# The even token mixer of a two-layer decoder trunk: one projection stream with heads and groups at fixed places

## The chip, the core and the metric

One of the eight cores of a Trainium2 chip runs the whole program. The metric is the device time of one execution in microseconds, the median of several runs; less is better. The engines are named PE (TensorE: matmuls, with PEld for its weight loads), DVE (VectorE), ACT (ScalarE), POOL (GpSimd) and SP (SyncE, which starts the weight DMAs). Each runs its own instructions in the order written and waits on semaphores for the others.

## The reference, cut to what matters

Tokens: 512. Width: 1024. The residual stream `x` passes six sub-layers, each `x += post(f(pre(x)))` with RMS norms: FFN, even mixer, FFN, FFN, odd mixer, FFN. The change touches the even mixer:

```python
q, k, v, g, a_low, z, xbc, dt = split(h @ w_in)
log_a = log_sigmoid(a_low @ w_gate2 + b_gate2) / 16
o = gla_chunked(q * 128**-0.5, k, v, log_a)          # 4 heads, key 128, value 256
o = rmsnorm(o, gla_norm) * silu(g)                   # per head
xbc = silu(causal_conv4(xbc)); xs, B, C = split(xbc) # 4 groups of 4 SSD heads of 64
dt = softplus(dt + dt_bias); a = -exp(a_log)
y = ssd_chunked(xs * dt, dt * a, B, C) + d * xs
y = rmsnorm(y * silu(z), ssm_norm)                   # per group of 256 columns
return concat([o, y]) @ w_out
```

All in float32. Both recurrences are computed in closed form over four blocks of 128 tokens, with decays `exp(b_i - b_j)`.

## The kernel before, in words

**Weights.** Every weight matrix is cut into slots of 128x1024. SP loads slot n into one of three `raw` buffers, ACT rounds it to `w_hi` (`split_high`, line 417), and DVE or POOL writes `w_lo = raw - w_hi` (`split_low`, lines 1231 and 354). PE forms each product as three matmuls (hi·hi, hi·lo, lo·hi) in the fast float32 format, `products` (line 784) with the weights stationary, `token_products` (line 793) with the weights moving. In the mixers a slot's split pair lies in a ring of four buffers (`INNER`), so slot n can be split once PE has finished slot n-4; elsewhere the ring has six. PE waits for `lo_done` before each slot. One slot of 24 matmuls with 512 columns is eight steps of three matmuls.

**The even mixer.** 49 slots are projected (`plan_stages`, line 52): 9 of `qk_small` (the small one holds `a_low` and `dt`), 8 of `v`, 16 of `xbc`, 16 of `zg`, and then 16 slots of `even_out`. PE does `first_four`, the rest of `qk_small`, `v`, `turn_dt` (line 951), then `gla_heads` (line 963) with the 16 `xbc` slots cut between the small products of four heads, `ssm_groups` (line 1011) with the 16 `zg` slots between those of four groups, and `sublayer_out` (line 848). `tiles_of` (line 895) deals the big matmuls: `project(2)` is two of the eight steps. A projected tile is copied from PSUM by DVE (`take`), and PE may not start the tile after the next before that. A head has seven levels of decays; level j needs DVE `differences(j)`, ACT `decay_of(j)`, DVE `factors(j)`, four PE matmuls and DVE `merge(j)`. The outputs of heads and groups are features x tokens, so that their norm needs sums over partitions: ACT squares, a DVE add, PE `norm_sums` (line 804), DVE mean, POOL power -0.5, a DVE diagonal, PE `norm_spread` (line 810), a DVE copy. POOL makes `w_lo` of all 49 slots from the fifth of the mixer to the fourth of `even_out`, in its own order, with the powers between (line 383). After the last group ACT and DVE split the 16 rows of the mixer's output into `cat_hi` and `cat_lo` (lines 566 and 1428), and PE starts `even_out` on them.

**The other sub-layers** run FFN slots back to back, with a `boundary` between two of them in which norms and transposes of one token chunk lie beside the matmuls of the next.

Of the kernel before, what the change touches and what calls it, by code (L numbers as in the profile page):

```python
# [7 lines left out]
F32 = mybir.dt.float32  # L8
# [24 lines left out]
DT0 = 32  # L33
# [18 lines left out]
def plan_stages():  # L52

    ffn = [[(f"gate_up{f}", 2 * FT), (f"down{f}", FT)] for f in range(N_FFN)]
    even = [("qk_small", 2 * GH + 1), ("v", 8), ("xbc", 16), ("zg", 16), ("even_out", 16)]
    odd = [("latent", 6), ("q_up", 5), ("k_up", 2), ("v_up", 2), ("odd_out", 8)]
    stages, first = {}, 0
    for name, slots in ffn[0] + even + ffn[1] + ffn[2] + odd + ffn[3]:
        stages[name] = (first, slots)
        first += slots  # L60
    return stages, first

def plan_ring(stages, total):
# [6 lines left out]
    for name in ("qk_small", "v", "xbc", "zg", "latent", "q_up", "k_up", "v_up"):  # L71
        inner |= set(range(stages[name][0], sum(stages[name])))
# [12 lines left out]
def plan_norms():  # L85

    names = [("gla", h) for h in range(GH)] + [("ssm", g) for g in range(SG)] + ["q_latent", "kv_latent"]
    return {name: n for n, name in enumerate(names)}

def build_trunk(nc, dram, out):
# [8 lines left out]
    with ExitStack() as ctx:  # L100
# [23 lines left out]
        v_head = [temps[:, 5 + c // 2, (c % 2) * GDV:(c % 2) * GDV + GDV] for c in range(NC)]  # L124
        diag = other[1].rearrange("p (c t) -> p c t", c=NC)

        gain_pre = sb("gain_pre", [P, D])
        mixer_misc, = parts(("mixer_misc", 1, D, F32))
        gain_post = sb("gain_post", [P, D])
        far_one, far_rest = temps[:, 7, 0:3 * P], mixer_misc[:, 0, 0:3 * P]  # L130
        far_blocks = [far_one, far_rest[:, 0:2 * P], far_rest[:, 2 * P:3 * P]]
        ssm_cols = mixer_misc[:, 0, 512:512 + 14 * SH].rearrange("p (n h) -> p n h", h=SH)

# [3 lines left out]
        mixer_cols = sb("mixer_cols", [P, 132])  # L137
# [13 lines left out]
        dt_bias = mixer_cols[DT0:DT0 + SH, 102:103]  # L151
        a_log = mixer_cols[DT0:DT0 + SH, 103:104]
# [8 lines left out]
        cat_lo, cat_hi = parts(("cat_lo", 24, T, F32R), ("cat_hi", 16, T, F32R))  # L161
# [26 lines left out]
        XS, B_ROWS, C_ROWS, Q, K, V = 0, 8, 12, 16, 20, 24  # L188
        CAT = [Q + h + m * GH for m in range(2) for h in range(GH)] + [XS + k for k in range(8)]
        small = rows(a_rows, 32)  # L190

        HALF_P = P // 2
        MASKS = len(SPANS) * HALF_P + P
        level_mask = rows(a_rows, 34)[:, 0:MASKS // 4].bitcast(U8)
        tri = rows(a_rows, 34)[:, 256:384]
        gate2 = rows(a_rows, 35)[0:RANK, :]
        LOG_A = 37
        head_rstd = rows(a_rows, 43)
        dt_rows, cum, far1, far2 = [rows(a_rows, n)[DT0:DT0 + SH, :] for n in (33, 32, 42, 43)]

        scores = rows(a_rows, 33).rearrange("p (c t) -> p c t", c=NC)
        k_dec = [rows(a_rows, 35 + b) for b in range(2)]
        conv_in = [rows(a_rows, 41 + b) for b in range(2)]

        cb = scores
        x_group = v_head
        x_far = rows(a_rows, 24, 3).rearrange("p (n v) -> p n v", n=6)
        decay = [rows(a_rows, 27 + b) for b in range(2)]
        from_start = [rows(a_rows, 29 + b) for b in range(2)]
        b_group = rows(a_rows, 31)  # L210
        xs_group = rows(a_rows, 35, 2).rearrange("p (m t) -> p m t", m=2)
        y_sum = [rows(a_rows, row) for row in (37, 39)]
        head_row = [rows(a_rows, 41 + b)[DT0:DT0 + SH, :] for b in range(2)]
# [9 lines left out]
        peak = mixer_cols[:, 112:116]  # L223
        peak_bias = mixer_cols[:, 116:120]
        prob_sum = mixer_cols[:, 120:124]
        chunk_decay = mixer_cols[:, 124:128]
        ssm_chunk_decay = mixer_cols[DT0:DT0 + SH, 128:132]
# [3 lines left out]
        SPLITS_BEFORE_NORM = {"xbc": 3, "zg": 2}  # L231
        XBC_BANKS, ZG_BANKS = (2, 3), (1, 6)
        QK0, V0, XBC0, ZG0, LATENT0 = 0, 9, 17, 33, 49

        def first_bank(n):

            return 4 + n if n < 4 else n % 4

# [19 lines left out]
        tile_taken, row_silu = sem("tile_taken"), sem("row_silu")  # L258
        conv_started, conv_step, conv_done = sem("conv_started"), sem("conv_step"), sem("conv_done")
        decay_logits, logit_ready, softplus_ready = sem("decay_logits"), sem("logit_ready"), sem("softplus_ready")  # L260
# [3 lines left out]
        key_copied, value_copied, gla_out = sem("key_copied"), sem("value_copied"), sem("gla_out")  # L264
        head_squares, head_summed = sem("head_squares"), sem("head_summed")
        dt_signal, dt_act, dt_cum, dt_far = sem("dt_signal"), sem("dt_act"), sem("dt_cum"), sem("dt_far")
        cols_turned, cols_ready = sem("cols_turned"), sem("cols_ready")
        group_copied, x_turned, x_taken, x_far_ready = sem("group_copied"), sem("x_turned"), sem("x_taken"), sem("x_far_ready")
        cb_ready, cb_taken, cb_far_taken = sem("cb_ready"), sem("cb_taken"), sem("cb_far_taken")
        head_row_ready, row_spread, from_start_ready = sem("head_row_ready"), sem("row_spread"), sem("from_start_ready")  # L270
        decay_diff, decay_exp, decay_ready = sem("decay_diff"), sem("decay_exp"), sem("decay_ready")
        y_diag_done, y_far_done, y_gated = sem("y_diag_done"), sem("y_far_done"), sem("y_gated")
        group_squares, group_summed, group_done = sem("group_squares"), sem("group_summed"), sem("group_done")
# [25 lines left out]
        ROW_BANKS = (0, 5)  # L299
        CB_AT = ((2, 0), (3, P), (5, 0), (5, 2 * P))  # L300
        FAR = [(0, 1), (1, 2), (2, 3), (0, 2), (1, 3), (0, 3)]

        @block.sync
        def _(sp):
# [9 lines left out]
            def load_gain_pre(s):  # L314
                sp.wait_ge(normed_ready, 8 * s)
                sp.dma_start(gain_pre[:, :], dram["gains"][s:s + 1, :].to_broadcast([P, D])).then_inc(gain_pre_in, 16)

            def load_gain_post(s):
                sp.wait_ge(update1_done, NC * s)
                if s == EVEN:  # L320
                    sp.wait_ge(group_done, SG)
# [9 lines left out]
            for s in range(N_SUB):  # L331
                names = [n for n in stages if first_slot[s] <= stages[n][0] < first_slot[s + 1]]
                for name in names:
                    first, slots = stages[name]
                    for n in range(RAW if first == 0 else 0, slots):
                        load(first + n, dram["w_" + name][n])
                        if first + n == first_slot[s] + 8 and s + 1 < N_SUB:
                            load_gain_pre(s + 1)
                        if s and first + n == {EVEN: last_slot[s] + 3, ODD: last_slot[s]}.get(s, first_slot[s] + 7):
# [9 lines left out]
        def _(pool):  # L349
# [27 lines left out]
            for b in range(N_SUB + 1):  # L377
# [5 lines left out]
                if b == EVEN:  # L383
                    split_some("qk_small", INNER, 9)
                    split_some("v", 0, 8)
                    split_some("xbc", 0, INNER)
                    for name, count, norm in (("xbc", GH, ("gla", 0)), ("zg", SG, ("ssm", 0))):
                        for turn in range(count):
                            for n in range(4):
                                if n == SPLITS_BEFORE_NORM[name]:  # L390
                                    power(turn + norms[norm])
                                split_low(stages[name][0] + INNER + 4 * turn + n)
# [13 lines left out]
        def _(act):  # L406
# [96 lines left out]
            def out_stage(s, ahead):  # L503

                n = last_slot[s] + ahead
                for j in range(max(2 * half_slots[s] - TAIL, half_slots[s] + 1)):
# [9 lines left out]
            def ffn(f, s):  # L516
# [8 lines left out]
                out_stage(s, RING)  # L525

            def even():
                def softplus(tile):
                    if tile == 4:
                        for h in range(GH):  # L530
                            act.wait_ge(logit_ready, h + 1)
                            after(nc.scalar.activation(other[h % 2], other[h % 2], ACT.Exp, scale=-1.0))
                            nc.scalar.activation(other[h % 2], other[h % 2], ACT.Ln, bias=1.0).then_inc(softplus_ready, 1)

                def step_sizes(tile):

                    if tile == 0:
                        act.wait_ge(dt_signal, 1)
                        nc.scalar.activation(far1, far1, ACT.Exp, scale=-1.0)
                        nc.scalar.activation(a_log, a_log, ACT.Exp).then_inc(dt_act, 1)  # L540
                    if tile == 1:
                        act.wait_ge(dt_signal, 2)
                        nc.scalar.activation(cum, far2, ACT.Ln).then_inc(dt_act, 1)
                    if tile == 2:
                        act.wait_ge(dt_cum, 1)
                        nc.scalar.activation(ssm_chunk_decay, cum[:, P - 1:T:P], ACT.Exp)
                        act.wait_ge(dt_cum, 2)
                        nc.scalar.activation(far1[:, 0:3 * P], far1[:, 0:3 * P], ACT.Exp).then_inc(dt_act, 1)

                first = first_slot[EVEN]  # L550
                for tile in range(9):
                    if tile == 8:
                        softplus(tile)
                    split_high(first + INNER + tile)
# [1356 lines left out]
```

## Time and profile before

| | |
|---|---|
| median of 3 runs | 2367.57 us (2367.52 to 2368.17) |
| the profiled execution, its own time | 2367.07 us |
| its span, and what lies around it | 2365.3 us, 1.8 us |
| busy: PE, PEld, DVE, ACT, POOL | 2239.2, 1812.3, 1009.8, 739.3, 193.0 us |
| mean granted PE clock | 0.967 |
| chain that ended last: PE, DVE, issue, ACT, POOL | 61%, 4%, 3%, 2%, 1% |
| DMA | 197.31 MB, mean 83 GB/s |

A busy PE is a PE with a matmul open; matmuls overlap, so a pace is read from the distance of two starts, not from one duration. The granted clock is 1.0 at 2.4 GHz and 0.5 at 1.2 GHz. The even mixer runs from the first matmul of its `first_four` at 387.6 us to that of the next FFN at 997.8 us.

### The profile page before, as it was taken

How to read it: one execution, taken by the hardware profiler on the slowest of the kernel's cores; microseconds unless marked ns; L12 is line 12 of the kernel's file. 1: busy time of each engine (PE TensorE's matmuls, PEld its weight loads, DVE VectorE, ACT ScalarE, POOL GpSimd, SP SyncE). 2: the span in 40 equal slices, each digit the busy share in tenths (PEclk: the TensorE clock that was granted, in tenths of full speed). 3: DMA queues.
4: the chain of work that ended last, by engine and by line, in shares of the span. 5: the costliest groups of instructions: out<-in, count | busy, mean ns of one | idle time of the engine just before them, and what ended most of it. 6: DMA issues, size and time to landing. Idle time of an engine off the chain costs nothing.

```text
span 2365.3 us, 25040 instructions
## 1 busy us (share of the span) xinstructions
PE 2239.2 (95%) x10358; PEld 1812.3 (77%) x10358; DVE 1009.8 (43%) x1438; ACT 739.3 (31%) x1141; POOL 193.0 (8%) x128
## 2 busy tenths in 40 slices
PE   7999999798888888999999999999998789999999
PEld 6888888677765666888888888888886348888887
DVE  4333224458876665443332343332265335333322
ACT  4222223433333333332221232222233434322211
POOL 0000001332212120000000000000033000000000
PEclk9999999899998889999999999999999779999999
DMA  5332332221111112242323232323222002332331
GB/s 180 95 102 89 107 98 71 79 71 45 54 36 37 43 36 101 69 134 89 107 89 107 72 125 92 104 89 107 90 83 75 15 0 71 118 106 89 107 98 54
DMA packets 55298, 197.31 MB, mean 83 GB/s; under 512 B 6272, under 2 KB 6784, under 8 KB 55184
## 3 DMA queue, kind: packets, MB, share of 16 engines
q1 hardware_dynamic: 53856, 193.75, 25.4%
q10 hardware_dynamic: 1328, 1.96, 0.2%
q8 instruction: 82, 1.34, 0.2%
q14 instruction: 32, 0.26, 0.0%
HBM read 193.58 MB, written 2.10 MB: 83 GB/s over the span
## 4 chain that ended last, share of the span: by engine, by line
PE 61%; DVE 4%; issue 3%; ACT 2%; POOL 1%; DVEq 0%; ACTq 0%; POOLq 0%
PE ps L789 11%; PE ps L790 11%; PE ps L791 11%; PE ps L797 7%; PE ps L799 7%; PE ps L798 7%; PE ps L1162 1%; PE ps L1161 1%; DVE a_rows L1226 1%; ACT a_rows L415 1%; ACT a_rows L727 1%; DVE a_rows L1223 1%; DVE temps L1223 1%; PE ps L1042 0%; PE ps L1172 0%
## 5 line engine op out<-in xcount | busy, mean ns | idle before, releaser
L789 PE MATMUL ps<-h_hi,w_hi 128*128 128x512 f32 (+1 forms) x1976 | 746.8, 378 | 12.4 <-DVE temps L1599 9.2
L791 PE MATMUL ps<-h_hi,w_lo 128*128 128x512 f32 (+1 forms) x1976 | 734.4, 372 | 0.0
L790 PE MATMUL ps<-h_lo,w_hi 128*128 128x512 f32 (+1 forms) x1976 | 733.9, 371 | 0.0
L415 ACT ACTIVATE w_hi<-raw 128x1024 fp32r<-128x1024 f32 x352 | 370.5, 1056 | 790.5 <-PE ps L799 392.4
L1223 DVE TENSOR_TENSOR w_lo<-raw,w_hi 128x1024 fp32r<-128x1024 f32 x288 | 343.7, 1221 | 338.0 <-ACT w_hi L415 337.4
L789 PEld LDWEIGHTS ps<-h_hi,w_hi 128*128 128x128 f32 x1976 | 376.4, 190 | 86.1 <-issue 21.1
L791 PEld LDWEIGHTS ps<-h_hi,w_lo 128*128 128x128 f32 x1976 | 376.2, 190 | 64.3
L790 PEld LDWEIGHTS ps<-h_lo,w_hi 128*128 128x128 f32 x1976 | 376.6, 191 | 61.8 <-issue 2.5
L1223 DVE TENSOR_TENSOR a_rows<-a_rows,ps 128x512 f32<-128x512 f32 x88 | 60.5, 688 | 614.0 <-PE ps L791 614.0
L797 PE MATMUL ps<-w_hi,a_hi 128*128 128x512 f32 x704 | 274.4, 390 | 0.0
L799 PE MATMUL ps<-w_hi,a_lo 128*128 128x512 f32 x704 | 274.0, 389 | 0.0
L798 PE MATMUL ps<-w_lo,a_hi 128*128 128x512 f32 x704 | 273.9, 389 | 0.0
L358 POOL TENSOR_TENSOR w_lo<-raw,w_hi 128x1024 fp32r<-128x1024 f32 x64 | 154.1, 2407 | 379.1 <-ACT w_hi L415 378.8
L799 PEld LDWEIGHTS ps<-w_hi,a_lo 128*128 128x128 f32 x704 | 132.1, 188 | 27.7
L798 PEld LDWEIGHTS ps<-w_lo,a_hi 128*128 128x128 f32 x704 | 132.2, 188 | 27.3
L797 PEld LDWEIGHTS ps<-w_hi,a_hi 128*128 128x128 f32 x704 | 132.1, 188 | 27.0
L520 ACT ACTIVATE a_rows<-ps 128x512 f32<-128x512 f32 x88 | 52.6, 598 | 317.6 <-PE ps L791 317.6
L371 POOL TENSOR_TENSOR stats<-stats,minus_half 128x1 f32<-128x1 f32 x24 | 13.2, 549 | 1613.8 <-DVE stats L1226 1613.8
L1223 DVE TENSOR_TENSOR a_lo<-a_rows,a_hi 128x512 fp32r<-128x512 f32 x88 | 60.3, 685 | 0.0
L1229 DVE SCALAR_TENSOR_TENSOR a_rows<-a_rows,mixer_cols 128x511 f32<-128x511 f32 (+3 forms) x61 | 54.5, 913 | 4.6 <-ACT a_rows L580 4.0
L797 PE MATMUL ps<-w_hi,cat_hi 128*128 128x512 f32 x128 | 50.7, 396 | 5.7 <-DVE cat_lo L1223 5.7
L415 ACT ACTIVATE a_hi<-a_rows 128x512 fp32r<-128x512 f32 x88 | 54.1, 615 | 0.0
(182 smaller groups left out, 1918.9 us busy)
## 6 DMA issues: line engine op xcount, KB each, us to landing
raw<-in_w_gate_up SPq DMA_DIRECT2D x176, 512.0 KB, 3.7
raw<-in_w_down SPq DMA_DIRECT2D x88, 512.0 KB, 3.5
raw<-in_w_xbc SPq DMA_DIRECT2D x16, 512.0 KB, 3.5
raw<-in_w_zg SPq DMA_DIRECT2D x16, 512.0 KB, 3.5
raw<-in_w_even_out SPq DMA_DIRECT2D x16, 512.0 KB, 3.6
raw<-in_w_qk_small SPq DMA_DIRECT2D x9, 512.0 KB, 3.5
raw<-in_w_v SPq DMA_DIRECT2D x8, 512.0 KB, 3.5
raw<-in_w_odd_out SPq DMA_DIRECT2D x8, 512.0 KB, 3.5
```

Of the source, the lines that this page charges most:

```text
L358: nc.gpsimd.tensor_tensor(w_lo[buffer_of[n]][:, 0:width], raw[n % RAW][:, 0:width], w_hi[buffer_of[n]][:, 0:width].bitcast(F32), ALU.subtr ...
L415: return nc.scalar.activation(to, source, ACT.Copy, scale=scale)
L520: nc.scalar.activation(rows(a_rows, tile), ps[:, (4 + 2 * tile) % 8, :], ACT.Silu).then_inc(silu_done, 1)
L727: nc.scalar.activation(probs[:, qt, 0:(qt + 1) * P], ps[:, qt, 0:(qt + 1) * P], ACT.Exp, bias=peak_bias[:, qt:qt + 1], scale=SCORE_SCALE, ...
L789: nc.tensor.matmul(to, w_h, hi, start=first, stop=False)
L790: nc.tensor.matmul(to, w_h, lo, start=False, stop=False)
L791: return nc.tensor.matmul(to, w_l, hi, start=False, stop=last)
L797: nc.tensor.matmul(ps[:, bank, :], hi, w_h, start=first, stop=False)
L798: nc.tensor.matmul(ps[:, bank, :], hi, w_l, start=False, stop=False)
L799: return nc.tensor.matmul(ps[:, bank, :], lo, w_h, start=False, stop=last)
L1223: return nc.vector.tensor_tensor(to, a, b, op)
L1229: return nc.vector.scalar_tensor_tensor(out=to, in0=a, scalar=scalar, in1=b, op0=op0, op1=op1)
```

## The change

The mixer's projections, and the first half of `even_out`, become one stream (a Python generator) whose steps of three 512-column matmuls are numbered: place -40 is the fifth slot of `qk_small`, 0 the first slot of `vg`, 320 the first of `even_out`, 384 its half. `plan_even` gives each head 41 places and each group 45, and each of their small products a place; `project_to(place)` runs the stream up to it. ACT and DVE ask `keep_up(place)` and so split slots, evict tiles and convolve up to that place, between the steps of heads and groups.

- The slot order is `qk_small`, `vg` (v and g by turns), `xbc` and `z` by groups. `v`, `g` and `z` are made tokens x features. `g` and `z` leave PSUM through ACT's Silu. `z2` and `z3` use matmuls of 256 columns.
- Heads and groups give tokens x features too. Their mean squares come from ACT with `accum_out`, the scale is one number per partition, and the result is transposed (eight per head or group) and split into `cat` straight from PSUM.
- The convolution reads PSUM itself: ACT writes the first tap, DVE adds three; the copies before it go.
- Each group's decays come from matmuls of `source_rows` and `head_rows` (32 rows deep) instead of `ones` times `head_row`; `skip` adds `d * xs` on PE.
- All `w_lo` of the mixer are made by DVE; POOL keeps the powers.
- The gains for the next sub-layer are loaded at slot 11 of `even_out`.

```diff
+    for h in range(GH):
+        base = 12 + 41 * h
+        for j, step in enumerate((0, 3, 7, 10, 14, 17, 22)):
+            at["level", h, j] = base + step
+        at["own", h], at["far", h], at["out", h], at["head_turn", h] = base + 25, base + 30, base + 36, base + 65
+    for g in range(SG):
+        base = 12 + 41 * GH + 45 * g
+        for name, step in (("x", 0), ("cb", 13), ("skip", 18), ("group_turn", 52)):
+            at[name, g] = base + step
+        for r in range(4):
+            at["decay", g, r] = base + (4, 9, 17, 22)[r]
+            at["near", g, r] = base + (19, 22, 27, 31)[r]
+    tile_end = [128 + 8 * (n + 1) + (32 if n >= 4 else 0) + (16 if n >= 12 else 0) for n in range(16)]
...
                 if b == EVEN:
-                    split_some("qk_small", INNER, 9)
...
+                    for n in range(GH + SG):
+                        power(n)
...
+                def split_to(place):
+                    while upcoming["slot"] < min(stream + place // 8 + 4, INNER_END):
+                        split_high(upcoming["slot"])
+                        upcoming["slot"] += 1
...
+                def keep_up(place):
+                    clear(place)
+                    for g in range(SG):
+                        if tile_end[4 * g + 1] + 3 <= place:
+                            silu_x(g)
+                        if tile_end[4 * g + 3] + 3 <= place:
+                            silu_bc(g)
+                    split_to(place)
...
+                    for j in range(len(SPANS)):
+                        keep_up(even_at["level", h, j] - AHEAD)
+                        decay_of(j)
...
+                    keep_up(max(even_at["near", g, 3] + 7, (192, 192, 272, 320)[g]))
+                    act.wait_ge(y_gated, g + 1)
...
+                        nc.scalar.activation(junk[c // 2][...], token_rows[c], ACT.Square,
+                                             scale=1.0 / 16.0, accum_out=group_sums[:, c:c + 1]).then_inc(group_squares, 1)
+                    act.wait_ge(rstd_col_ready, norms[("ssm", g)] + 1)
+                    for c in range(NC):
+                        copy(token_rows[c], token_rows[c], rstd_col[:, c:c + 1]).then_inc(y_scaled, 1)
...
+                def project_to(place):
+                    while placed[0] < place:
+                        next(projecting)
+                        placed[0] += 1
...
+                    for j in range(len(SPANS)):
+                        project_to(even_at["level", h, j])
+                        pe.wait_ge(gla_factors, h * 8 + (j + 1))
...
+                    def decays(r):
+                        n = 4 * g + r
+                        project_to(even_at["decay", g, r])
+                        pe.wait_ge(head_row_ready, n + 1)
...
+                    decays(0)
+                    project_to(even_at["x", g] + 7)
+                    turn_group(g - 1) if g else turn_head(GH - 1)
+                    decays(1)
...
+                        if j == 2 and h + 1 < GH:
+                            log_decay(h + 1)
+                        if j == 3 and h == 0:
+                            step_sizes()
...
+                    keep_up(even_at["near", g, 3] + 7)
+                    pair = token_pair.rearrange("p (c v) -> p c v", c=2)
+                    dve.wait_ge(y_far_done, g + 1)
...
+                    tt(pair, pair, z_pair(g), ALU.mult).then_inc(y_gated, 1)
+                    dve.wait_ge(group_squares, 4 * g + 4)
+                    ts(mean[:, :], group_sums, EPS, None, ALU.add).then_inc(mean_ready, 1)
```

## Rows read from the trace of the kernel before

**Rows 1.** The chain of waits by engine, from the page.
```profile
PE 61%; DVE 4%; issue 3%; ACT 2%; POOL 1%; DVEq 0%; ACTq 0%; POOLq 0%
```

**Rows 2.** Busy time by stretch: each engine's busy us and records, PE clock, DMA share.
```profile
core 0: us, PE busy (x) PEld busy (x) DVE busy (x) ACT busy (x) POOL busy (x), PEclk, DMA share, GB/s
387.60:505.00 117.40, 103.50 (x529) 86.47 (x527) 50.02 (x72) 43.91 (x52) 40.38 (x19) 0.94 0.27 85
...
509.30:692.00 182.70, 162.91 (x849) 132.84 (x850) 153.28 (x259) 60.74 (x101) 42.80 (x20) 0.95 0.15 47
692.00:907.40 215.40, 177.55 (x737) 125.06 (x735) 135.35 (x240) 74.17 (x111) 42.79 (x20) 0.87 0.12 37
907.40:997.70 90.30, 90.25 (x400) 74.85 (x401) 40.30 (x56) 30.35 (x54) 2.96 (x6) 0.98 0.30 99
387.60:997.70 610.10, 538.06 (x2541) 422.92 (x2540) 381.83 (x630) 211.45 (x322) 131.28 (x66) 0.92 0.19 59
```

**Rows 3.** PE by form, 345 to 1010 us: busy, mean ns, idle before, releaser.
```profile
L789 PE MATMUL ps<-h_hi,w_hi 128*128 128x512 f32 x296 | 131.6, 445 | 9.7 <-DVE temps L1599 9.2 <-DVE mixer_misc L1423 0.5
...
L797 PE MATMUL ps<-w_hi,cat_hi 128*128 128x512 f32 x128 | 50.7, 396 | 5.7 <-DVE cat_lo L1223 5.7
...
L976 PE MATMUL ps<-temps,a_rows 128*128 128x64 f32 x224 | 31.5, 288 | 8.2 <-DVE a_rows L1223 7.7 <-DVE a_rows L1527 0.5
...
L1042 PE MATMUL ps<-a_rows,ones 16*128 16x512 f32 x32 | 19.8, 721 | 0.0
L812 PE MATMUL ps<-temps,ones 128*128 128x512 f32 x16 | 10.9, 768 | 16.0 <-DVE temps L1223 16.0
...
L807 PE MATMUL ps<-ones,temps 128*128 128x1 f32 x64 | 8.4, 252 | 5.4 <-DVE temps L1223 5.4
```

**Rows 4.** PE's timeline: start us, duration us, what; pace of the big matmuls.
```profile
503.58 0.39 PE L797 MATMUL ps<-w_hi,h_hi 128*128 128x512 f32 x1
...
504.26 0.39 PE L797 MATMUL ps<-w_hi,h_hi 128*128 128x512 f32 x1
...
997.77 0.28 PE L789 MATMUL ps<-h_hi,w_hi 128*128 128x256 f32 x1
...
998.13 0.28 PE L789 MATMUL ps<-h_hi,w_hi 128*128 128x256 f32 x1
```

**Rows 5.** PE's timeline: the small products and what starts after them.
```profile
519.56 1.00 PE L976 MATMUL ps<-temps,a_rows 128*128 128x64 f32 x8
520.37 0.48 PE L789 MATMUL ps<-h_hi,w_hi 128*128 128x512 f32 x1
...
753.09 1.03 PE L1021 MATMUL ps<-ident,a_rows 128*128 128x128 f32 x8
753.96 2.32 PE L1025 MATMUL ps<-a_rows 128*128 128x512 f32 x8
756.04 0.48 PE L789 MATMUL ps<-h_hi,w_hi 128*128 128x512 f32 x1
...
780.69 0.71 PE L1059 MATMUL ps<-temps,a_rows 128*128 128x128 f32 x4
...
782.23 1.09 PE L1050 MATMUL ps<-a_rows,temps 128*64 128x128 f32 x8
783.25 0.50 PE L789 MATMUL ps<-h_hi,w_hi 128*128 128x512 f32 x1
```

**Rows 6.** POOL by form, 387 to 998 us.
```profile
L358 POOL TENSOR_TENSOR w_lo<-raw,w_hi 128x1024 fp32r<-128x1024 f32 x49 | 119.0, 2429 | 323.8 <-ACT w_hi L415 323.6
L367 POOL TENSOR_TENSOR rstd_col<-mean,minus_half 128x4 f32<-128x4 f32 x8 | 8.1, 1009 | 61.2 <-DVE mean L1226 61.2
```

**Rows 7.** DVE: two row operations in the timeline, and two forms.
```profile
596.65 0.68 DVE L1223 TENSOR_TENSOR temps<-ident,rstd_col 128x512 f32<-128x512 f32 x1
597.25 2.71 DVE L1226 TENSOR_SCALAR a_rows<-a_rows,mixer_cols 128x512 f32<-128x512 f32 x1
...
L1223 DVE TENSOR_TENSOR w_lo<-raw,w_hi 128x1024 fp32r<-128x1024 f32 x23 | 28.0, 1223 | 58.2 <-ACT w_hi L415 58.0
...
L1416 DVE TENSOR_TENSOR_SCAN a_rows<-ones,a_rows 128x128 f32<-128x128 f32 x16 | 10.8, 748 | 0.0
```

**Rows 8.** ACT by form, 345 to 1010 us.
```profile
L415 ACT ACTIVATE w_hi<-raw 128x1024 fp32r<-128x1024 f32 x73 | 76.3, 1052 | 134.9 <-PE ps L799 98.6 <-PE ps L791 29.0 <-DMA raw<-in_w_v 4.2
L586 ACT ACTIVATE temps<-temps 128x512 f32<-128x512 f32 x28 | 17.6, 629 | 55.0 <-DVE temps L1223 54.9
...
L632 ACT ACT_TABLE_LOAD x4 | 5.1, 1283 | 0.1
```

More of the change, by code:

```diff
@@ L208, in build_trunk @@
[L208 to L213, printed above, removed]
+        masks_in = rows(a_rows, 34, 2)[:, 0:MASKS]
+        level_mask = early_rows[:, 0, 0:MASKS // 4].bitcast(U8)
+        tri = early_rows[:, 0, 144:272]
@@ L524, in ffn @@
                     copy(rows(a_hi, tile), rows(a_rows, FT + tile)).then_inc(a_hi_ready, 1)
-                out_stage(s, RING)
+                out_stage(s, last_slot[s] + RING)
             def even():
[L528 to L548, printed above, removed]
@@ new lines, in even @@
+                nc.scalar.activation(exp_cum, cum_early, ACT.Exp)
+                act.wait_ge(dt_cum, 2)
+                nc.scalar.activation(far1[:, 0:3 * P], far1[:, 0:3 * P], ACT.Exp).then_inc(dt_act, 1)
+                for h in range(1, GH):
+                    head(h)
+                for g in range(SG):
+                    group(g)
+                turn_group(SG - 1)
+                act.wait_ge(group_squares, 4 * SG)
+                out_stage(EVEN, upcoming["slot"], (even_at["group_turn", SG - 1] - 320) // 8)
@@ L1071, in ssm_groups @@
+                    near(2)
+                    near(3)
                     pe.wait_ge(x_far_ready, g + 1)
[L1072 to L1083 removed]
@@ L1086, in odd @@
+                for g in range(SG):
+                    group(g)
+                project_to(even_at["group_turn", SG - 1])
+                turn_group(SG - 1)
+                for _ in projecting:
+                    pass
+                second_half(s, block_source)
             def odd():
@@ L1406, in even @@
[L1406 to L1415 removed]
+                first = first_slot[EVEN]
@@ new lines, in even @@
+                for buffer in k_dec:
+                    nc.vector.memset(buffer, 0.0)
+                after(nc.vector.memset(temps[:, 6, :], 0.0))
+                dve.wait_ge(dt_act, 1)
+                ts(far2, far1, 1.0, None, ALU.add).then_inc(dt_signal, 1)
+                logits()
+                split_to(-32)
+                split_to(-24)
+                dve.wait_ge(softplus_ready, 1)
+                log_decay(0)
+                split_to(-16)
+                split_to(-8)
+                for h in range(GH):
+                    head(h)
```

1175 lines of the change are left out of this document (650 added, 525 removed).

## The prediction

> **What bounds the kernel now.** I read three views in this order. The chain of waits comes first: PE has 61% of it and no other engine over 4% [rows 1], so PE sets the end and the question is how well it is fed. The busy time by stretch comes second [rows 2]: in the even mixer, 610.1 us long, PE is busy 538.06 us, so it is idle 72.0 us, and its mean granted clock is 0.92. A clock of 0.92 means that 8% of the stretch's full-speed cycles are missing, 0.08 x 610.1 = 48.8 us. Part of the slow time is idle anyway, so this is an upper bound of what the clock costs. What is left is work at full clock: 610.1 - 72.0 - 48.8 = 489.3 us. By stage 13.9 us are idle in the first projections, 19.8 in the heads, 37.9 in the groups (clock 0.87), and nearly nothing in the output. The third view, PE by form, says what the idle time ends with [rows 3]: 16.0 us before `norm_spread`, 5.4 before `norm_sums`, 9.2 for a copy of a `zg` tile, 8.2 before level products, 5.7 before the output. These are waits for DVE, whose own steps sit in one long row behind one another.
>
> A step of three big matmuls at full clock is 504.26 - 503.58 = 0.68 us [rows 4]. I call that a place; a slot is 5.4 us.
>
> **PE's own work.** The big matmuls are the same: 49 + 16 slots. `z2` and `z3` need 192 matmuls of 256 columns in place of 96 of 512; three of them take 0.36 us against 0.68 for three wide ones [rows 4], so 64 x 0.36 - 32 x 0.68 = +1.2 us.
> Each head and each group loses `norm_sums` and `norm_spread`. By form they take 8.4 / 8 = 1.05 and 10.9 / 8 = 1.36 us, slow clock included [rows 3]; at full clock I take 0.9 and 0.95, an estimate from the 0.81 to 1.02 us that a group of four small products costs [rows 5]. They gain eight transposes, 753.96 - 753.09 = 0.87 us [rows 5]. That is -1.0 us, eight times: -8.
> In a group the four `near` products shrink from 128 to 64 moving columns: from 783.25 - 782.23 = 1.02 to the 520.37 - 519.56 = 0.81 us of a level [rows 5], -0.8 together. The far products keep their 1536 columns (782.23 - 780.69 = 1.54 us for half of them), taken as no change. The decays are 4 x 512 columns before and after: before, 32 records took 19.8 us with slow clock, 1.24 per 512 columns [rows 3]; after, the like of a `near`, 1.02, is the nearest row. At full clock I take no change, with bounds of -1 and +1 us a group. `skip` is new: 1024 columns, at the price of the 1280 of `cb` in 756.04 - 753.96 = 2.08 us [rows 5], +1.7. A group: +0.9 us, four times +3.6.
> Sum: 1.2 - 8 + 3.6 = about -3, with bounds -8 and +3. (One head is then 7 levels x 0.81, 0.9, 1.5, 4.2 for 2560 columns at the price of `cb`, and 0.9: 13 us; a group 15.) I take 486 us of work.
>
> **DVE's load.** The change gives DVE 49 subtractions of 1.22 us, 60 us [rows 7], which POOL did in 2.43 us each [rows 6]. But POOL's were not free for DVE. A row operation of DVE takes 0.68 us; the one that starts at 597.25, while POOL's subtraction runs, takes 2.71 [rows 7]. So a POOL split costs DVE up to 2.03 us when it hits such an operation, and DVE's own costs 1.22. Over 49 slots the move is worth between +60 us of DVE time (if none was hit) and -40 (if all were). Between them I take -10, nearer to the row that shows the hit.
> The Trainium skill, page "Perfetto Trace Analysis", section "Optimizing Scalar/DVE Operations", says that offloading to GPSIMD may make sense where DVE is saturated; by that alone this part of the change is a step back, worth +60 us on DVE. The same passage warns that the two share an SBUF read port, and the page "SBUF — State Buffer", section "Who interferes with whom", has a two-input DVE instruction contend with a GpSimd one that reads SBUF, the loser blocked for the whole instruction. The trace agrees with this: 2.71 against 0.68 us.
> DVE also loses, per head or group, the tile copies, the square sum, the diagonal (all 0.68) and the final products, and it gets three taps per tile as before. In a head I count 28 half rows and 7 merges at 0.34, half of 0.68 (12), the eighth merge and the key factors (3), `log_decay` (3.7), gate and cat (2.6), 5.1 splits (6.2): 27 us, and 31 in head 0. In a group 16 rows (10.9), 9 taps (6.3), 5.6 splits (6.9), and 4 for the end: 28. A head lasts 41 x 0.68 + 13 = 41 us on PE and a group 45 x 0.68 + 15 = 46. No engine but PE is the bound by sums; what remains is order.
>
> **The waits that are left,** each from a chain between fixed places.
> - Start. PE reaches level 0 of head 0 at place 12, 8.2 us after place 0. DVE must have the logits, the softplus from ACT, the first `log_decay` (one row operation and four scans of 0.75 [rows 7], 3.7 us) and four splits behind it. I find it 2 to 3 us late: 3.
> - Head 0, places 12 to 22. PE takes 10 x 0.68 + 3 x 0.81 = 9.2 us. DVE has three levels' differences and factors (12 half rows: 4 us), two merges (1), `log_decay(1)` (3.7), `step_sizes` (five row operations and four scans, 6.5) and a split (1.2): 16.4. Late: 7.
> - Heads 1 to 3. Level 0 waits for ACT, which after `gla_out` squares four blocks (4 x 0.6, not over the 0.63 of a full row [rows 8]) before its exponential; level 2 waits behind `log_decay`. 2 us each: 6, and 1 for `turn_dt`.
> - From one group to the next. `decays(0)` of the next group waits for ACT's `head_row(0)`, which in ACT's order stands behind the whole end of the last group. After the far products: convolution of the next tile (0.6 + 3 x 0.7), a Silu with its table load (1.28 + 1.05 [rows 8]), a split by ACT and DVE (1.05 + 1.2), seven DVE operations (3.6), four squares (2.4), the mean and POOL's power (0.2 + 1.0 [rows 6]), four scaled copies (1.6), `head_row` (0.6): 15.7, and about 1.5 for the handovers: 17. PE has places 31 to 49, 18 x 0.68 = 12.2, and 0.9 of transposes: 13.1. Late 4 us, three times: 12.
> - Within a group, the table loads between Silu and Exp before `cb`: 1.5 us each: 6.
> - After the last group ACT and DVE can split slot 6 of `even_out` only then, since its buffer lies on `temps`: 2.
> Sum: 3 + 7 + 7 + 12 + 6 + 2 = 37 us, where 72.0 were. The wait before the output and those for the norms go, because their results are due only at later places. The bounds are 12 (most handovers hide, as each estimate adds a chain in full) and 90 (each handover costs more than I give it).
>
> **The clock.** Before, 48.8 us are lost beside 72.0 idle, 0.68 per us of idle time. For 37 us that is 25. The Trainium skill, "TensorE: Matmul & The Clock Gate", section "HAM oscillation — how this bites in real kernels", also ties the reduced clock to gaps in PE's work; the trace agrees in that the stage with the most idle time has 0.87 [rows 2] and the gapless output 0.98.
>
> **Sum.** Mixer after: 486 + 37 + 25 = 548 us, against 610.1: -62. Against the profiled execution, 2367.1 - 62 = 2305; its own time is 0.5 us under the median of the runs, so the median comes to 2305.5 too. The other sub-layers stay. The post gain is now loaded behind slot 11 of `even_out`, which SP may issue once slot 9 is split, at about place 376; DVE wants it at 384, and while DVE waits PE has split slots for a dozen places: 0, and up to +5 if that cover fails.
>
> **The rivals.**
> 1. The places fit as planned and waits nearly vanish: 12 us of waits, 8 of clock, 506: -104, 2263. For it: DVE and ACT have a third of their time free. Against: `head_row` behind `y_scaled` is in the order of the program.
> 2. Half of it: waits of 60 us with 41 of clock, 587: -23, 2344. For it: every `keep_up` makes DVE and ACT wait for PE's place, so a late chain is not caught up before the next.
> 3. The other side: the fixed places make DVE and ACT the bound. PE, ACT and DVE then pass each place one after the other, because an engine that waits for slot n-4 of a ring of four in `split_high` has its decay or Silu queued behind it. The price is the full latency of each handover: 11 us lost per head and group, 88 in all, with 60 of clock, 634: +24, 2391. It decides from 75 us of waits on (75 x 1.68 = 126 > 610 - 486 = 124), 9.4 us per head and group. For it: ACT waits 134.9 us before its splits already [rows 8]. Against: those waits are on PE, which is the bound, and cost nothing now.
> 4. The new order does not reach PE's waits at all (they were due to weights or DMA): 2367. DMA is at 19% of its time in the mixer [rows 2], so I give it next to nothing.
>
> **How the numbers follow.** Forecast 0.62, rival 1 0.17, rival 2 0.12, rival 3 0.07, rival 4 0.02. The forecast's own range is 2280 to 2330. For 8 in 10 it reaches to rival 1 below and rival 2 above: 2262 to 2345. A measurement of this kernel tells 0.2%, 4.7 us, from no change. Faster: 0.62 + 0.17 + 0.12 = 0.91; within: 0.02; slower: 0.07.
>
> **What would show it.** Right: the mixer lasts about 548 us with under 45 us idle, a clock near 0.96, no POOL subtraction in it, no DVE row operation of 2.7 us, `even_out` starting without a gap. PE's longest waits are at level 3 of head 0 and at `decays(0)` of groups 1 to 3. Wrong: PE waiting for `w_lo` at slots, a clock still at 0.92 with little idle time, small products that cost more than 1.1 us per 512 columns, or DVE busy over 85% of the heads.

## The result and the profile after

The changed kernel takes 2350.66 us (median of 4 runs, 2349.26 to 2352.83). The kernel before, on the same chip, takes 2367.87. The ratio is 0.9928, with a 95% interval of 0.9911 to 0.9945. It is faster, but by 17 us where 62 were forecast, and outside the range of 2262 to 2345. The profiled execution took 2349.26 us, its span is 2347.5.

The mixer did what was forecast. The stages, each measured from its first projection matmul to the next stage's first one, in the profiled executions:

| stage | before | after | difference |
|---|---|---|---|
| up to the mixer's first matmul | 387.6 | 397.5 | +9.9 |
| even mixer (forecast 548) | 610.2 | 547.1 | -63.1 |
| the second and third feed-forward | 728.4 | 749.4 | +21.0 |
| odd mixer | 270.9 | 274.9 | +3.9 |
| last feed-forward, to the end | 368.1 | 378.7 | +10.5 |

So 63 us were gained in the mixer and 45 lost everywhere else, where the diff changes no matmul. First the mixer by stretch: engines' busy us and records, clock, DMA share, to be held against [rows 2]. The cuts lie about where head 0 is under way, where the heads end and where `even_out` begins.
```profile
core 0: us, PE busy (x) PEld busy (x) DVE busy (x) ACT busy (x) POOL busy (x), PEclk, DMA share, GB/s
397.50:515.00 117.50, 113.36 (x621) 95.36 (x620) 67.03 (x125) 47.86 (x74) 2.28 (x4) 0.99 0.27 80
515.00:678.00 163.00, 156.90 (x831) 129.86 (x830) 94.38 (x196) 75.37 (x123) 3.02 (x3) 0.99 0.17 55
678.00:839.30 161.30, 140.17 (x780) 119.43 (x779) 83.95 (x126) 78.29 (x120) 3.02 (x3) 0.94 0.16 49
839.30:944.50 105.20, 105.14 (x498) 85.98 (x499) 43.44 (x61) 36.07 (x69) 4.11 (x7) 1.00 0.29 90
397.50:944.50 547.00, 515.57 (x2725) 430.64 (x2724) 288.80 (x504) 237.60 (x384) 12.43 (x17) 0.98 0.21 66
```
PE is idle 547.0 - 515.6 = 31.4 us (37 forecast, 72.0 before). DVE falls from 381.8 to 288.8 us although it now makes every `w_lo`. POOL has no subtraction left.

Next, what PE waits for in the mixer: engine and line, what it waited for, us in total, times, longest.
```profile
PE ps L1237 <- ACT a_rows L732: 8.8, 3, 3.1
PE ps L1181 <- DVE temps L1456: 6.8, 6, 2.5
PE ps L941 <- ACT a_rows L635: 3.8, 2, 3.0
PE ps L1258 <- DVE early_rows L1456: 3.4, 2, 2.3
PE ps L1285 <- DVE temps L1456: 2.7, 1, 2.7
PE ps L1246 <- DVE temps L1456: 2.3, 2, 1.2
```
L1237 is `decays`, L732 `head_row`, L1181 a level of a head, L635 the Silu of a `z` tile: the longest waits stand where the prediction put them, three times at `decays(0)` (8.8 us for 12 forecast). The longest level wait is at level 3 of head 0, as forecast too:
```profile
477.75 1.10 PE L1181 MATMUL ps<-temps 128*128 128x64 f32 x8 [2.52 <-DVE temps L1456]
```

Last, the loss outside. PE's timeline in the first feed-forward, 300 us before any changed step, of the kernel after:
```profile
99.63 0.40 PE L941 MATMUL ps<-h_hi,w_hi 128*128 128x512 f32 x1
99.87 0.40 PE L942 MATMUL ps<-h_lo,w_hi 128*128 128x512 f32 x1
100.11 0.39 PE L943 MATMUL ps<-h_hi,w_lo 128*128 128x512 f32 x1
100.34 0.40 PE L941 MATMUL ps<-h_hi,w_hi 128*128 128x512 f32 x1
```
Three matmuls start in 0.71 us, not in the 0.68 of [rows 4]. How many PE starts in 200 us without a gap shows it better. The same stretches of the kernel before (busy PE, then its records in brackets):
```profile
50.00:250.00 200.00, 200.00 (x885) 165.58 (x883) 66.47 (x75) 57.91 (x75) 0.00 (x0) 1.00 0.31 99
290.00:380.00 90.00, 90.00 (x399) 74.52 (x398) 25.88 (x30) 21.27 (x34) 1.65 (x3) 1.00 0.28 88
```
and of the kernel after:
```profile
50.00:250.00 200.00, 200.00 (x855) 160.82 (x854) 61.99 (x70) 54.67 (x70) 0.00 (x0) 1.00 0.30 95
290.00:380.00 90.00, 90.00 (x387) 72.39 (x386) 22.13 (x22) 19.56 (x26) 0.00 (x0) 1.00 0.30 94
```
PE is busy all the time at full clock in both (PEclk 1.00), and nothing waits. Yet 855 matmuls fit where 885 did. From start to start, the 512-column matmuls of gate/up take 234.3 ns in place of 226.7 (means over that stretch; down products take 233.3 in place of 226.7 in the second one). No other engine and no transfer is the cause: 275 of the 852 distances in the kernel after hold neither DVE nor ACT work nor a DMA packet, and their mean is 234.3 ns too. The first stretch is gate/up (stationary `h_hi`/`h_lo`, moving weights), the second down (stationary weights, moving `a_hi`/`a_lo`).

One line of the diff reaches all stages:
```
-        mixer_cols = sb("mixer_cols", [P, 132])
+        mixer_cols = sb("mixer_cols", [P, 172])
```
### The profile page after: what moved, and what is told of

Same layout as the page of the kernel before. It is cut to its first block, busy times and chain, and to the rows that moved or that the text cites. A ratio compares the mean times of both kernels' runs of the same rounds, so it can differ in the third digit from the quotient of the medians.

```text
span 2347.5 us, 25279 instructions
## 1 busy us (share of the span) xinstructions
PE 2262.9 (96%) x10542; PEld 1822.3 (78%) x10542; DVE 914.6 (39%) x1312; ACT 766.7 (33%) x1204; POOL 74.4 (3%) x79
## 4 chain that ended last, share of the span: by engine, by line
PE 87%; DVE 6%; ACT 4%; issue 2%; DMA 0%; POOL 0%; SPq 0%; DVEq 0%; ACTq 0%
PE ps L941 16%; PE ps L943 16%; PE ps L942 16%; PE ps L951 9%; PE ps L950 9%; PE ps L949 9%; PE ps L1395 1%; PE ps L1394 1%; DVE a_rows L1462 1%; PE ps L1105 1%; DVE w_lo L1456 1%; PE ps L1106 1%; PE ps L1107 1%; PE ps L1181 1%; PE ps L1218 1%
## 5 line engine op out<-in xcount | busy, mean ns | idle before, releaser
L941 PE MATMUL ps<-h_hi,w_hi 128*128 128x512 f32 (+1 forms) x1848 | 696.0, 377 | 6.8 <-ACT a_rows L635 3.8
L943 PE MATMUL ps<-h_hi,w_lo 128*128 128x512 f32 (+1 forms) x1848 | 690.8, 374 | 0.0
L942 PE MATMUL ps<-h_lo,w_hi 128*128 128x512 f32 (+1 forms) x1848 | 690.5, 374 | 0.0
L1456 DVE TENSOR_TENSOR w_lo<-raw,w_hi 128x1024 fp32r<-128x1024 f32 x337 | 402.8, 1220 | 384.0 <-ACT w_hi L478 383.3
L941 PEld LDWEIGHTS ps<-h_hi,w_hi 128*128 128x128 f32 x1848 | 349.8, 189 | 77.1 <-ACT a_rows L635 4.5
L942 PEld LDWEIGHTS ps<-h_lo,w_hi 128*128 128x128 f32 x1848 | 350.1, 189 | 65.7
L950 PE MATMUL ps<-w_lo,a_hi 128*128 128x512 f32 x704 | 277.4, 394 | 0.0
L1105 PE MATMUL ps<-w_hi,h_hi 128*128 128x512 f32 (+1 forms) x224 | 87.0, 388 | 1.5 <-DVE a_rows L1462 1.0
L1107 PE MATMUL ps<-w_hi,h_lo 128*128 128x512 f32 (+1 forms) x224 | 82.9, 370 | 0.0
L1106 PE MATMUL ps<-w_lo,h_hi 128*128 128x512 f32 (+1 forms) x224 | 82.9, 370 | 0.0
L478 ACT ACTIVATE a_rows<-ps 128x512 f32<-128x512 f32 (+1 forms) x68 | 32.0, 520 | 91.5 <-PE ps L1405 58.1
```

What stands on the lines that cost most here:

```text
L478: return nc.scalar.activation(to, source, ACT.Copy, scale=scale)
L941: nc.tensor.matmul(to, w_h, hi, start=first, stop=False)
L942: nc.tensor.matmul(to, w_h, lo, start=False, stop=False)
L943: return nc.tensor.matmul(to, w_l, hi, start=False, stop=last)
L950: nc.tensor.matmul(ps[:, bank, :], hi, w_l, start=False, stop=False)
L1105: nc.tensor.matmul(to, h_hi[:, block, cols], w_hi[b][:, of], start=block == 0, stop=False)
```

## The experiments

"Before" in each result is the kernel before on the same chip.

**1. The kernel after, operands back in line.**
```
-        mixer_cols = sb("mixer_cols", [P, 172])
+        mixer_cols = sb("mixer_cols", [P, 196])
```

> The changed kernel with one edit: mixer_cols has 196 columns instead of 172, so every tensor behind it in SBUF (h_hi, h_lo, a_rows, a_hi, a_lo) starts 96 bytes later, at an address divisible by 128 as before the change; after the change it is 32 off. Theory A (the address slows the matmuls): FFN matmuls with 512 columns start every 226.7 ns again instead of 234.3; some 7800 of them x 7.6 ns = 59 us less, 2291 us. Theory B (the chip, or the larger program, slows the matmuls): no change, 2350 us, pace 234.3. Theory C (the new order of the mixer leaves the engines in a state that slows what follows): no change either, but then the first FFN, which runs before the mixer, should not be slow.

Measured: 2297.44 us (2296.15 to 2303.36), before 2366.35, ratio 0.9716 (0.9702 to 0.9731). The two stretches again, of this kernel:
```profile
50.00:250.00 200.00, 200.00 (x884) 165.65 (x883) 66.19 (x75) 57.47 (x75) 0.00 (x0) 1.00 0.31 99
290.00:380.00 90.00, 90.00 (x398) 74.51 (x398) 25.81 (x31) 21.29 (x34) 1.65 (x3) 1.00 0.29 88
```
The old pace is back. The mixer is 544.6 us long; its row:
```profile
387.30:931.80 544.50, 511.64 (x2725) 431.79 (x2724) 288.88 (x504) 237.36 (x384) 12.43 (x17) 0.97 0.21 66
```
Another 96 unused bytes are worth about 50 us (the two ratios differ by 0.0212), three times what the change as made gained. The expectation, 7800 matmuls x 7.6 ns = 59 us, was too large by 9; experiment 2 shows where.

**2. The kernel before with the same line alone.**
```
-        mixer_cols = sb("mixer_cols", [P, 132])
+        mixer_cols = sb("mixer_cols", [P, 172])
```

> The kernel before with one edit: mixer_cols has 172 columns instead of 132, which moves everything behind it by 160 bytes, as in the changed kernel, and nothing else. Theory A: pace of the 512-column matmuls 234.3 ns instead of 226.7, some 7800 x 7.6 = 59 us more, 2427 us. Theory B and C: 2368 us, pace 226.7.

Measured: 2414.47 us (2412.03 to 2417.61), before 2366.35, ratio 1.0204 (1.0187 to 1.0221). The width of this one buffer costs 48 us by itself. In the profiled execution the four feed-forwards have 42 of it, the even mixer 5 (615.2 for 610.2) and the odd one 2 (273.2 for 270.9). The 59 expected counted the mixers' matmuls in full, but PE waits there for other engines as well.

**3 and 4. Other distances.** 148 and 140 columns move the same region by 64 and by 32 bytes.

> The kernel before, moved by 64 bytes (mixer_cols with 148 columns). If A holds and 64 bytes is the grain that matters: 2368 us, pace 226.7. If 128 is the grain: slower, pace near 234.

> The kernel before, moved by 32 bytes (mixer_cols with 140 columns). If A holds with a grain of 64 or 128: as b_160, about 2427 us, pace 234.3. If 160 bytes matter for another reason than their rest by 64 or 128: 2368 us.

Measured, a single run each: 2392.13 and 2409.34 us. The same stretches, by 64 bytes:
```profile
50.00:250.00 200.00, 200.00 (x875) 164.09 (x874) 65.70 (x74) 56.57 (x73) 0.00 (x0) 1.00 0.30 98
290.00:380.00 90.00, 90.00 (x387) 72.12 (x386) 23.35 (x26) 20.56 (x31) 1.10 (x2) 1.00 0.28 88
```
and by 32:
```profile
50.00:250.00 200.00, 200.00 (x858) 160.61 (x857) 62.64 (x71) 56.00 (x72) 0.00 (x0) 1.00 0.29 95
290.00:380.00 90.00, 90.00 (x388) 72.44 (x387) 22.51 (x22) 19.23 (x26) 0.21 (x1) 1.00 0.30 94
```
By 32 both kinds are slow. By 64 the down products are as slow (387) and gate/up loses a third as much (875 of 885). So neither of the two outcomes expected for 64 bytes came in full: it depends on which operand is the stationary one.

**5. Everything moved together:** 32 unused bytes ahead of `x`, so that both operands leave 32 when divided by 128 and their distance stays.
```
+        sb("front", [P, 8])
         x = sb("x", [P, NC, D])
```

> The kernel before with 32 unused bytes ahead of the first tensor, so that every tensor, the weights' w_hi and w_lo too, is moved by 32 bytes and all keep their distances. If the slow matmul comes from the address itself (theory A1): as in b_32 or worse, 512-column pace about 233 ns or more, 2409 us or more. If it comes from the distance between the two operands that PE reads at a time (theory A2): pace 226.7, 2366 us.

Measured, a single run: 2369.52 us beside 2363.57 of before (2362.94 to 2368.16).
```profile
50.00:250.00 200.00, 200.00 (x884) 165.63 (x884) 66.86 (x75) 57.88 (x74) 0.00 (x0) 1.00 0.30 98
290.00:380.00 90.00, 90.00 (x399) 74.55 (x398) 26.30 (x30) 20.85 (x33) 1.65 (x3) 1.00 0.28 88
```
The pace is the old one, though this time lies 1.4 us above the highest of the seven runs of before. So it is not where an operand begins, but how far TensorE's two operands lie apart.

**6. Only the down operand moved:** 32 unused bytes between `h_lo` and `a_rows`.
```
+        sb("between", [P, 8])
```

> The kernel before with 32 unused bytes between h_lo and the region of a_rows: gate and up read h and w at their old addresses, the down products read a_hi and a_lo moved by 32 as stationary operand and w at its old address as moving one. A1 and A2 both: gate and up 226.7 ns, down about 233; 2112 down matmuls x 6.6 = 14 us, with the mixers' outputs 18 us: 2384 us. If the program's other tensors (mixer_cols, stats, the ones behind) were the cause: no change.

Measured, a single run: 2391.58 us.
```profile
50.00:250.00 200.00, 200.00 (x884) 165.67 (x883) 67.00 (x75) 57.85 (x74) 0.00 (x0) 1.00 0.30 98
290.00:380.00 90.00, 90.00 (x387) 72.49 (x386) 23.64 (x26) 20.30 (x31) 1.23 (x3) 1.00 0.29 88
```
One program, two paces: gate/up keeps 884, down falls to 387, and only down's operand moved. The cost follows the pair. The time is 28 us over before (24 between the two profiled executions) where 18 were expected: the down products give 14 as expected, but the even mixer has 6 more (616.3 us) and the odd one 4 (274.8). The small products read the moved `a_rows` there, and no run separates what they cost.

**7. The kernel before, with the mixer's `w_lo` made by DVE** in DVE's old order; POOL keeps only the powers.
```
 block.gpsimd:
-                    split_some("qk_small", INNER, 9)
...
-                                split_low(stages[name][0] + INNER + 4 * turn + n)
+                    for n in range(GH + SG):
+                        power(n)
 block.vector, four places in each head and group:
+                    split_low(stages["xbc"][0] + INNER + 4 * h + 1)
```

> The kernel before with one part of the change alone: the 49 w_lo of the mixer made by DVE, in its old order, instead of POOL. My theory (a POOL subtraction holds back a DVE operation by up to 2.0 us, a split costs DVE 1.2): DVE's long operations of 2.7 us go, the mixer gets some 5 to 20 us shorter, 2350 to 2361 us. Rival (DVE is what PE waits for, and gets 60 us more): the mixer gets longer by 10 to 40 us.

Measured: 2324.95 us (2322.51 to 2325.64), before 2363.57, ratio 0.9829 (0.9815 to 0.9844). This part alone is worth 39 us, more than my theory gave it; the rival had the sign wrong. DVE in 162 us of the heads, 505 to 667 us, by form; the kernel before:
```profile
L1223 DVE TENSOR_TENSOR temps<-a_rows 128x256 f32<-128x256 f32 x56 | 29.3, 570 | 0.2
L1229 DVE SCALAR_TENSOR_TENSOR a_rows<-a_rows,mixer_cols 128x510 f32<-128x510 f32 x13 | 16.0, 1227 | 0.1
...
L1226 DVE TENSOR_SCALAR a_rows<-a_rows,mixer_cols 128x512 f32<-128x512 f32 x3 | 8.1, 2714 | 0.0
...
L1223 DVE TENSOR_TENSOR a_rows<-a_rows,temps 128x384 f32<-128x384 f32 x3 | 7.7, 2560 | 0.1
```
and this one:
```profile
L1216 DVE TENSOR_TENSOR temps<-a_rows 128x256 f32<-128x256 f32 x56 | 20.8, 418 | 0.2
L1216 DVE TENSOR_TENSOR w_lo<-raw,w_hi 128x1024 fp32r<-128x1024 f32 x15 | 18.2, 1216 | 0.0
...
L1222 DVE SCALAR_TENSOR_TENSOR a_rows<-a_rows,mixer_cols 128x510 f32<-128x510 f32 x13 | 9.7, 744 | 0.1
...
L1216 DVE TENSOR_TENSOR a_rows<-a_rows,temps 128x384 f32<-128x384 f32 x4 | 2.2, 558 | 0.1
...
L1219 DVE TENSOR_SCALAR a_rows<-a_rows,mixer_cols 128x512 f32<-128x512 f32 x3 | 1.6, 541 | 0.0
```
In the kernel before, beside POOL's 14 subtractions in this stretch, four kinds of DVE step were 8.5 + 6.3 + 6.5 + 6.0 = 27 us longer (56 x 0.152, 13 x 0.483, 3 x 2.17, 3 x 2.00; e.g. 2714 ns for 541). DVE's own 15 cost 18.2. The meeting in time can be seen inside the kernel before: of its 56 `128x256` steps `temps<-a_rows` in the mixer the 52 that meet no subtraction of POOL take 416 ns, the 4 that meet one 2562. Copies from PSUM aren't held (`a_rows<-ps`: 684 ns without, 685 with).

The gain is in the groups. The heads take 182.7 us before [rows 2] and 174.1 here, the groups 215.4 and 180.3. PE's waits in the groups, before (692 to 907.5 us):
```profile
PE ps L812 <- DVE temps L1223: 10.5, 4, 2.7
PE ps L789 <- DVE temps L1599: 9.2, 4, 2.4
PE ps L797 <- DVE cat_lo L1223: 5.7, 1, 5.7
```
and here (684.6 to 865):
```profile
PE ps L790 <- DVE cat_lo L1216: 5.0, 1, 5.0
...
PE ps L805 <- DVE temps L1216: 0.9, 2, 0.6
PE ps L782 <- DVE temps L1608: 0.8, 3, 0.3
```
The norm's spread (10.5 us before, 0.9 here) and the tile copy (9.2 and 0.8) are hardly waited for now. Behind the power of each group POOL goes on to a subtraction, and DVE's diagonal, which the spread needs, meets it and takes 2.83 us; the same step takes 0.69 here:
```profile
792.36 1.01 POOL L367 TENSOR_TENSOR rstd_col<-mean,minus_half 128x4 f32<-128x4 f32 x1 [11.72 <-DVE mean L1226]
793.33 2.34 POOL L358 TENSOR_TENSOR w_lo<-raw,w_hi 128x1024 fp32r<-128x1024 f32 x1
...
793.40 2.83 DVE L1223 TENSOR_TENSOR temps<-ident,rstd_col 128x512 f32<-128x512 f32 x1 [1.12 <-POOL rstd_col L367]
...
796.28 1.12 PE L812 MATMUL ps<-temps,ones 128*128 128x512 f32 x2 [2.71 <-DVE temps L1223]
```
Two successive powers of the groups stand 792.36 - 738.87 = 53.5 us apart before and 765.14 - 722.23 = 42.9 here. The groups have 18.6 us idle at a clock of 0.96; before they had 37.9 at 0.87 [rows 2]:
```profile
684.60:864.90 180.30, 161.71 (x738) 114.50 (x736) 123.16 (x255) 72.92 (x108) 4.03 (x4) 0.96 0.14 43
```

**8. The new order, with the splits given back to POOL** (on top of experiment 1), each power placed between them. "The new order" stands for all of the change but who makes `w_lo`.
```
 block.gpsimd:
+                            split_low(n)
...
+                        power(turn)
 block.vector:
-                        split_low(upcoming["slot"])
```

> The changed kernel with aligned operands (a_pad, 2297 us), with the mixer's w_lo given back to POOL and nothing for DVE in their place. My theory: DVE operations stretch to 2.7 us where they meet POOL, the waits of PE in heads and groups grow, 5 to 25 us slower, 2302 to 2322 us. Rival (DVE is relieved of 56 us and PE's waits for DVE shrink): 2285 to 2295 us.

Measured: 2294.09 us (2293.27 to 2295.06), before 2363.57, ratio 0.9700 (0.9684 to 0.9716), beside 0.9716 (0.9702 to 0.9731) with DVE's splits. My expectation failed: they are equal within their intervals. The number lies in the rival's range, but DVE is relieved of 11.5 us in the mixer (277.4 for 288.9), not of 56. DVE's steps are stretched here too, 684 ns for 419 in this row of the heads (500 to 661 us):
```profile
L1464 DVE TENSOR_TENSOR temps<-a_rows 128x256 f32<-128x256 f32 x38 | 24.3, 684 | 0.1
```
but in the new order that reaches PE little: its waits for level products grow from 7.5 to 12.5 us, those for `head_row` fall from 9.1 to 4.2. So the 39 us of experiment 7 and the gain of the rest of the change don't add up: the rest alone, with POOL's splits, has the whole of it.

**9. Experiment 1, with ACT's `head_row(0)` and `(1)` of the next group ahead of its wait for the gated rows.**
```
+                    if g + 1 < SG:
+                        head_row(0, g + 1)
+                        head_row(1, g + 1)
                     keep_up(max(even_at["near", g, 3] + 7, (192, 192, 272, 320)[g]))
                     act.wait_ge(y_gated, g + 1)
```

> The kernel after with mixer_cols widened to 196 columns, and ACT's first two head rows of groups 1 to 3 issued ahead of its wait for the gated rows of the group before, where they stood behind the scaled rows of that group. The work is the same. Theory: the three waits of PE on ACT for those rows (3.1 us each, 9.1 together in the kernel with 196 columns alone) end only because of ACT's order; they go, and PE gains 9 us and 1 to 4 more by its clock, which fell to 0.95 over the stretch that holds them: 2284 to 2290 where the kernel with 196 columns alone took 2297. Rival 1: PE then waits for the next thing of the same turn, the scaled rows or the exponentials (1 to 2 us each), and half of the gain stays: 2291 to 2294. Rival 2: the head rows now stand ahead of the squares on ACT and delay the norm of each group by 0.5 us twice: 2296 to 2300.

Measured: 2293.53 us (2292.87 to 2298.66), before 2366.84, ratio 0.9699 (0.9685 to 0.9712); its interval overlaps that of experiment 1. PE's waits in the mixer:
```profile
PE ps L1185 <- DVE temps L1460: 7.5, 8, 2.6
PE ps L945 <- ACT a_rows L635: 5.5, 2, 4.7
PE ps L1262 <- DVE early_rows L1460: 3.4, 2, 2.3
PE ps L1275 <- ACT a_rows L662: 3.2, 1, 3.2
```
The waits for `head_row` are gone (9.1 us). In their place PE waits up to 4.7 us for the Silu of a `z` tile (L635; 3.0 in experiment 1) and 3.2 for that of the `b` and `c` rows ahead of `cb` (L662; 0.4), both ACT's. The number lies in the range of rival 1, but the waits aren't those that it named, the scaled rows or the exponentials. By the medians 4 us came of it, which the intervals don't tell from nothing, and in the profiled execution (2298.66 us, the slowest of the five) the mixer lasts 544.2 us beside 544.6 in experiment 1. The theory of 2284 to 2290 failed.

**10. Experiments 8 and 9 together.**

> The same early head rows, and POOL makes the mixer's w_lo as in the kernel where it was given back to it (2294.1 beside 2363.6 of the kernel before, a ratio of 0.9700). There the waits for head rows were 4.2 us in two, and the longest were for DVE's temps in the heads (12.5 us in five). Theory: only 4 us and a little clock can be gained: 2287 to 2290. Rival: with POOL's splits beside DVE's steps the heads wait as before and the groups gain nothing: 2293 to 2296, so that this kernel ends behind the one where DVE splits.

Measured: 2288.53 us (2286.22 to 2291.43), before 2366.84, ratio 0.9675 (0.9662 to 0.9688). This is within the 2287 to 2290 of the theory. Its waits for `head_row` are gone too, and its mixer lasts 534.5 us. It is the fastest kernel of the study, 78 us under the kernel before. Against experiment 1 its interval is clear of overlap; against experiment 8 or 9 it is not. But all its four times lie under all five of experiment 9 on the same chip (2292.87 and up).

## Why the prediction was wrong, and where it was right

**The step that failed** is "The other sub-layers stay", and with it the place: "A step of three big matmuls at full clock is 504.26 - 503.58 = 0.68 us". I took the pace of an unchanged matmul as fixed, and counted a wider small buffer as nothing. It is 234.3 ns, not 226.7. A feed-forward has 1152 matmuls of gate/up, 192 of them with 256 columns (+7.0 us from the first start to the last, 249.5 for 242.5), and 528 of down (+3.4, 124.7 for 121.3), four times: 42 us; with the odd mixer (+3.9) that is the 45 us of the table. Experiments 1 and 2 show it from both sides (-50 with the distance restored, +48 with it alone disturbed), and 5 and 6 show that the distance between the pair decides. No rival held it either: all four were about the mixer, and the "+5" for the other stages was an argument about one load. The diff's line on `mixer_cols` was there to be read; but no row of the trace before could price it.

**The mixer's sum held:** 548 forecast, 547.1 measured, and 544.6 at the old pace. With the operands in line the whole kernel takes 2297.44, 8 us from the forecast. Its terms at the old pace (row of experiment 1): idle 544.5 - 511.6 = 32.9 (37 forecast); clock 0.03 x 544.5 = 16 (25 forecast); the work left is 495 (486 forecast). So my three terms were off by -4, -9 and +9, and the good total owes something to that. The clock term fell more than in proportion to idle time: 16 / 32.9 = 0.5 per us, against 0.68 before. The clock is known to two digits, so it moves 3 us between these two terms. The work's +9 I can't place among the small products.

**Waits.** The chain from group to group was the right one, but 8.8 us for 12. It was also summed wrongly: its steps add up to 16.7 us and not 15.7, which makes 15 of the 12. Levels of the heads, head 0 among them, cost 6.8 in all, the longest 2.52 where I had 7 for head 0 alone: my chains were added in full though parts of them overlap. Projections of the groups wait 3.8 us for the Silu of a `z` tile on ACT, which I had not seen. Of the 5.7 us before the output [rows 3] nothing is left, as forecast.

**DVE and POOL.** "Between them I take -10" was an estimate of DVE's time. In the old order the move took 17 us off it (364.6 us busy in the mixer of experiment 7 for 381.8 before), which fits, and 39 off the kernel, which the term didn't say. In the new order, where I used it, the sign is the other one: DVE is busy 288.9 us with its own splits and 277.4 with POOL's, and the kernel's time doesn't tell them apart (experiment 8). The row behind the estimate compared two kinds of step, 2.71 us for a `TENSOR_SCALAR` and 0.68 for a `TENSOR_TENSOR`; the first kind alone takes 541 ns. That steps of DVE are held for about the length of POOL's is also what the Trainium skill has in "SBUF — State Buffer", section "Who interferes with whom": the loser of the shared port is held for the whole instruction. The trace agrees: 2714 - 541 = 2.17 us beside a subtraction of 2.38.

What the splits gave the old order was slack on a chain that the new order keeps off PE's path anyway. That sentence is read from the waits and not shown; a kernel with POOL busy but its results unused, which would separate the stretching from the delivery of `w_lo`, was not tried. Nor was the rest of the change taken apart: how much of its gain is the fixed places, and how much the new layout, the norms without `norm_spread` or the convolution from PSUM, stays open.

**Rivals.** Rival 2's time, 2344, is near the measured one by chance: its cause, waits of 60 us, is not there. Rival 1's 12 us of waits aren't either, and rival 4 is out, as the idle time fell from 72.0 to 31.4 us. Rival 3 is out: DVE is busy 58% of the heads (94.38 of 163), and the longest wait is 3.1 us. The odd mixer, which was not changed, takes 266.4 us in experiment 1 and 270.9 before. This is no effect of the change: in the four kernels of the new order with operands in line it takes 266.4 to 270.9 us, in experiment 7 271.6. What it varies with stays open.

## What to carry to other kernels

And an engine's stretched steps cost the kernel only as long as they are on the chain that PE waits for, so a part's worth measured in the old order isn't its worth in the new one.

## What the runs showed of the hardware

- The pace of 512-column matmuls in the fast float32 format (`fp32r` in the rows) depends on how far apart the stationary and the moving operand begin in SBUF. The distances of starts below are means over the two stretches without a gap, at a granted clock of 1.00. At the old distance and with 256 bytes more (experiment 1): 226.7 ns. With 32 more: 233.3 for both kinds of product. With 160 more: 233.3 with the weights stationary, 234.3 with the weights moving. With 64 more: 233.3 with the weights stationary, 228.9 with the weights moving.
- A rest by 128 bytes is the simplest rule that fits these, as 160 acts nearly as 32 does, but a rest by 256 fits as well: no run moved an operand by 128.
- The products of 256 columns show no such loss: 119.9 ns before, 118.1 after.
- It isn't the address itself: with both operands moved by 32 bytes the pace stays at 226.7 ns. The Trainium skill, "SBUF — State Buffer", section "Who interferes with whom", calls TensorE's two read ports, for the moving operand and for the weights, independent. These runs show a dependence that it doesn't name; why the distance matters stays open.
- One POOL subtraction of 128x1024 can hold a DVE step of 0.54 us for 2.7. In 162 us of the heads 14 of them made four kinds of DVE step 27 us longer.
